# MLP down projection as seven half-size products per 1024 up columns (Strassen's scheme)

## The chip, the cores and the metric

The kernel runs on one core of one Trainium2 chip. The metric is the device time of one execution in microseconds (us). It is written in Bass, with every engine's instruction stream and every semaphore wait written out by hand. The engines are PE (TensorE, matmuls), PEld (its weight loads), DVE (VectorE), ACT (ScalarE), POOL (GpSimd) and SP (SyncE, which issues most DMAs).

## The reference

A decoder layer on 512 tokens of width 1024: three attention branches, a gated merge, cross-attention, and an MLP. The change touches the MLP alone. There `x` is (512, 1024), `mlp_w1` (1024, 4096) and `mlp_w2` (4096, 1024), all float32:

```python
h = rmsnorm(x, g[NORM_PRE_MLP])
x = x + rmsnorm(jnp.square(jax.nn.relu(h @ mlp_w1[l])) @ mlp_w2[l], g[NORM_POST_MLP])
```

## The kernel before, in words

Every dense product is done in three TensorE passes. Each float32 operand is split into a high part (rounded to the fp32r type) and a low part (the rest), and `blocks3` (L688 to L693) issues high times high, high times low and low times high for each 128-row chunk, all added up in PSUM. Each is a matmul of 128x128 stationary by 512 moving columns in most stages.

The weights come in slabs of 1 MB (128 partitions by 2048 columns). SP loads slab s into `raw[s % 2]` as soon as slab s-2 has been split (`load`, L640 to L643). ACT writes the high part (`high`, through the copy helper at L1333) into `wh[s % 2]` once TensorE is through with slab s-2, and VectorE subtracts it from the raw slab to give the low part (`low`, L1823 for slabs in halves or quarters, L1828 for whole ones) in `wl[s % 2]`. A "halved" slab is handed over in two halves, so that TensorE can begin on the first.

The MLP runs in two rounds (f = 0, 1) of 2048 up columns. A round has eight up slabs of 256 columns (48 matmuls each) and then eight down slabs (2 column halves of the output by 4 groups of 512 up columns, 48 matmuls each). For each up product ACT takes relu out of PSUM into `h1` (L1776), GpSimd squares it in place (L2463), ACT copies the high part to `h1H` (L1333, `up_high`), and VectorE writes the low part to `h1L` (L2355). ACT evicts the down products of round 0 to `yN`; VectorE adds those of round 1 (L2371). The row norm then follows for each 128-token tile: ACT squares and sums a half row (L1633), VectorE multiplies by the gain (L2374, L2390), adds the two sums (L2235), ACT takes the root (L1645), VectorE the reciprocal (L2377), and two fused multiply-adds (L2380, L2383) write the output rows that SP stores (L673).

Engines execute their streams strictly in the order written. So a wait in front of one instruction holds all that stand behind it on that engine. The order on VectorE in an up step is: low part of up slab n+2, then low part of up product n-1. ACT's is: relu of n, high part of slab n+2, high part of up product n-1.

Of the kernel before, what the change touches and what calls it, by code (L numbers as in the profile page):

```python
# [24 lines left out]
F32 = mybir.dt.float32  # L25
# [6 lines left out]
P = 128  # L32
# [49 lines left out]
def layer(nc, a, out):  # L82
# [11 lines left out]
    with ctx:  # L94
# [65 lines left out]
        gainPost = [at("gain_post0", [P, D], 172), at("gain_post1", [P, D], 180), at("gain_post2", [P, D], 176)]  # L160
        gainPre = [at("gain_pre0", [P, D], 176), at("gain_pre1", [P, D], 172)]
        squareJunk = at("square_junk", [P, D], 202)
        scaled = at("y_scaled", [P, NT, T], 160)
# [13 lines left out]
        h1H = at("up_high", [P, 16, T], 96, F32R)  # L177
        h1L = at("up_low", [P, 16, T], 128, F32R)
        h1 = at("up", [P, 2, 2, T], 160)
# [43 lines left out]
        CROSS = [S[0], PT, OT, S[1]]  # L223

# [105 lines left out]
        for f in range(2):  # L330
            for n in range(8):
                c = f * 2048 + n * SW
                slab(("up", f, n), square_slab(rows("mlp_w1"), c, c + SW))
            for n in range(2):
                for kk in range(4):
                    row_slab(("down", f, n, kk), rows("mlp_w2"), n, kk, f * 16)
# [3 lines left out]
        for s, pieces in enumerate(slabs):  # L340
            counts[s % 2] += 16 * len(pieces)
            landed.append(counts[s % 2])

# [5 lines left out]
                                              ("up", 0, 0), ("up", 0, 1))}  # L349
# [3 lines left out]
                                                        ("bp", 1, 3), ("nq", 0), ("kk", 0), ("vv", 0))})  # L353

# [123 lines left out]
        for f in range(2):  # L478
            for n in range(8):
                product(("up", f, n), "A", slab_at["up", f, n])  # L480
            for n in range(2):
                for kk in range(2):
                    part(slab_at["down", f, n, kk])
                if f == 0 or n == 0:
                    part(slab_at["down", f, n, 2])
                for t in range(NT):
                    if f == 1 and n == 1 and t == NT - 1:
                        part(slab_at["down", f, n, 2])
                    product(("down", f, n, t), "A" if f == 0 else "V", slab_at["down", f, n, 3])
# [14 lines left out]
        place_free[slab_at["up", 0, 1]] = used_at[slab_at["co", 1, 0]]  # L504
# [6 lines left out]
        def row_rank(name, n, t):  # L511

            return 4 * (t // 2) + 2 * n + t % 2 if name == ("co",) else NT * n + t
# [83 lines left out]
        gains2_loaded = sem("gain_rows_loaded_again")  # L597
        row_squared = [sem(f"row_squares{j}") for j in range(3)]
# [36 lines left out]
        def _(sp):  # L635
# [32 lines left out]
            for s in range(slab_at["cw", 0, 0], SLABS):  # L668
                load(s)
            for t in range(NT):  # L670
                for n in (1, 0):
                    sp.wait_ge(out_ready, 2 * t + 2 - n)
                    sp.dma_start(out_row(out)[:, t, n * T:(n + 1) * T], XN[:, t, n * T:(n + 1) * T]).then_inc(out_written, 16)  # L673
# [4 lines left out]
        def _(pe):  # L678
# [602 lines left out]
            def up_half(n, half, at_chunk=None):  # L1281

                c = slice(half * 2 * P, (half + 1) * 2 * P)
                act = (hTH[:, :, c], hTL[:, :, c])
                g = product_at["up", 0, n]
                dst = [G[g % 2][:, b, c] for b in range(2)]
                pe.wait_ge(taken["V"], taken_count[product_at["co", n, NT - 1]])
                return t_mode(slab_at["up", 0, n], dst, both, KD, act, at_chunk)
# [9 lines left out]
            up = (h1H, h1L)  # L1298
            for f in range(2):
                for n in range(0 if f else 2, 8):  # L1300
                    g = product_at["up", f, n]
                    if n < 2:
                        pe.wait_ge(taken["A"], taken_count[product_at["down", 0, 1, 2 * n + 1]])
                    else:
                        free(g)
                    t_mode(slab_at["up", f, n], two(g), both, KD, hT).then_inc(product_ready, 1)
                for n in range(2):
                    name = ("down", f)
                    together = f == 1 and n == 1
                    for kk in range(2 if together else 4):  # L1310
                        pe.wait_ge(up_ready, 8 * f + 2 * kk + 2)
                        for t in range(NT):
                            if kk == 0:
                                free_tile(name, n, t)
                            mm = rows_tile(slab_at["down", f, n, kk], name, n, t, up, 4 * kk, kk == 0, kk == 3)
                            if kk == 3 or t == NT - 1:
                                mm.then_inc(product_ready, 1)
                    if together:
                        for t, kk in ((0, 2), (1, 2), (0, 3), (1, 3), (2, 2), (2, 3), (3, 2), (3, 3)):
# [1164 lines left out]
```

## Time and profile before

| | us |
|---|---|
| median of 3 runs | 1449.33 |
| lowest and highest run | 1448.76, 1449.4 |
| span of the profiled execution, first to last instruction | 1447.3 |

The runs' time includes about 2.0 us around the span (1449.33 - 1447.3). The profile's page gives no other time for the profiled execution, so its own time is taken as its span and these 2.0 us.

| engine | busy us in the span | share |
|---|---|---|
| PE | 1435.3 | 99% |
| PEld | 1169.0 | 81% |
| DVE | 694.2 | 48% |
| ACT | 567.1 | 39% |
| POOL | 93.8 | 6% |

A matmul's listed duration reaches from its start until its result is out. Matmuls overlap, so what one of them costs in a full stream is the distance from one start to the next. The duration of a group on DVE or ACT is what an instruction takes, time in which it stands blocked after dispatch included.

### The profile page before, as it was taken

The numbers are of one execution on the slowest core, as the hardware profiler recorded it, in microseconds if no ns is written. First come the engines' busy times: TensorE is split into PE (matmuls) and PEld (weight loads), VectorE is DVE, ScalarE is ACT, GpSimd is POOL, SyncE is SP. The second block draws the span as 40 slices with busy tenths as digits, with TensorE's granted clock in tenths as the row PEclk, the third lists the DMA queues.
The fourth block names the chain that finished last, engine by engine and source line by source line (L and its number), as shares of the span: only waits on it lengthen the run. The fifth ranks groups of instructions, "written<-read, shape, count | busy, mean of one in ns | idle before, by whom it ended". The sixth has DMA issues, their size and how long they took to land.

```text
span 1447.3 us, 17264 instructions
## 1 busy us (share of the span) xinstructions
PE 1435.3 (99%) x7138; PEld 1169.0 (81%) x7138; DVE 694.2 (48%) x1194; ACT 567.1 (39%) x935; POOL 93.8 (6%) x70
## 2 busy tenths in 40 slices
PE   9999999999999999999999999999999999999998
PEld 7867778888888888877767888987789888888886
DVE  6477857854333454556155345563454232123234
ACT  4455541234334333355356234444434332233221
POOL 0000000023020000100000110000001110011100
PEclk9999999999999999999999999999999999999999
DMA  6211233223221245531100533452122322322321
GB/s 200 68 41 35 70 105 100 88 91 99 73 88 59 95 141 175 157 97 44 59 29 30 189 105 103 143 188 74 58 65 86 113 87 89 115 87 88 116 87 58
DMA packets 118144, 137.34 MB, mean 95 GB/s; under 512 B 7044, under 2 KB 98433, under 8 KB 118066
## 3 DMA queue, kind: packets, MB, share of 16 engines
q1 hardware_dynamic: 115216, 126.17, 27.2%
q0 software_dynamic: 2704, 10.00, 2.0%
q8 instruction: 57, 0.93, 0.3%
q14 instruction: 21, 0.17, 0.0%
q10 hardware_dynamic: 146, 0.07, 0.0%
HBM read 134.09 MB, written 2.14 MB: 94 GB/s over the span
## 4 chain that ended last, share of the span: by engine, by line
PE 98%; DVE 1%; ACT 0%; DMA 0%; issue 0%; DVEq 0%; ACTq 0%
PE dense L691 26%; PE dense L693 26%; PE dense L692 26%; PE score L837 4%; PE score L854 3%; PE turned L854 3%; PE turned L837 2%; PE turned L847 1%; PE score L847 1%; PE score L1008 1%; PE score L1009 1%; PE score L1231 0%; PE turned L1231 0%; PE score L1220 0%; PE turned L1220 0%; PE turned L819 0%
## 5 line engine op out<-in xcount | busy, mean ns | idle before, releaser
L1828 DVE TENSOR_TENSOR weight_low<-raw,weight_high 128x2048 fp32r<-128x2048 f32 (+2 forms) x96 | 200.2, 2092 | 356.1 <-ACT weight_high L1333 356.0
L691 PE MATMUL dense<-hidden_high,weight_high 128*128 128x512 f32 (+1 forms) x840 | 327.0, 389 | 0.0
L1333 ACT ACTIVATE weight_high<-raw 128x2048 fp32r<-128x2048 f32 (+5 forms) x172 | 222.2, 1323 | 259.9 <-PE dense L693 259.7
L693 PE MATMUL dense<-hidden_high,weight_low 128*128 128x512 f32 (+1 forms) x840 | 320.7, 382 | 0.0
L692 PE MATMUL dense<-hidden_low,weight_high 128*128 128x512 f32 (+1 forms) x840 | 320.3, 381 | 0.0
L693 PEld LDWEIGHTS dense<-hidden_high,weight_low 128*128 128x128 f32 x840 | 157.9, 188 | 30.9
L692 PEld LDWEIGHTS dense<-hidden_low,weight_high 128*128 128x128 f32 x840 | 158.2, 188 | 29.1 <-issue 0.5
L691 PEld LDWEIGHTS dense<-hidden_high,weight_high 128*128 128x128 f32 x840 | 158.1, 188 | 29.0 <-issue 0.5
L1823 DVE TENSOR_TENSOR weight_low<-raw,weight_high 128x1024 fp32r<-128x1024 f32 (+1 forms) x74 | 76.0, 1078 | 60.6 <-ACT weight_high L1333 60.6
L691 PE MATMUL dense<-weight_high,up_high 128*128 128x512 f32 x256 | 99.6, 389 | 0.0
L692 PE MATMUL dense<-weight_low,up_high 128*128 128x512 f32 x256 | 99.6, 389 | 0.0
L693 PE MATMUL dense<-weight_high,up_low 128*128 128x512 f32 x256 | 99.6, 389 | 0.0
L691 PE MATMUL dense<-weight_high,hidden_high 128*128 128x256 f32 (+1 forms) x288 | 82.0, 285 | 0.3 <-DVE hidden_low L1854 0.2
L693 PE MATMUL dense<-weight_high,hidden_low 128*128 128x256 f32 (+1 forms) x288 | 81.2, 282 | 0.0
L692 PE MATMUL dense<-weight_low,hidden_high 128*128 128x256 f32 (+1 forms) x288 | 81.2, 282 | 0.0
L691 PE MATMUL dense<-branch_out_high,weight_high 128*128 128x512 f32 x192 | 75.0, 391 | 0.0
L1446 ACT ACTIVATE probs<-probs,small 128x128 f32<-128x128 f32 (+3 forms) x128 | 70.2, 551 | 11.9 <-DVE small L1998 11.7
L693 PE MATMUL dense<-branch_out_high,weight_low 128*128 128x512 f32 x192 | 74.8, 389 | 0.0
L692 PE MATMUL dense<-branch_out_low,weight_high 128*128 128x512 f32 x192 | 74.7, 389 | 0.0
L1776 ACT ACTIVATE up<-dense 128x1024 f32<-128x1024 f32 x16 | 16.5, 1029 | 112.4 <-PE dense L693 112.4
L1333 ACT ACTIVATE probsT<-turned 128x512 f32<-128x512 f32 (+4 forms) x68 | 32.0, 471 | 71.5 <-PE turned L847 71.2
L837 PE MATMUL score<-kT,qT 128*128 128x128 f32 (+3 forms) x174 | 57.8, 440 | 0.7 <-ACT index_relu L1427 0.4
(341 smaller groups left out, 2288.9 us busy)
## 6 DMA issues: line engine op xcount, KB each, us to landing
raw<-in_w_in SPq DMA_DIRECT2D x33, 1024.0 KB, 5.2
raw<-in_mlp_w SPq DMA_DIRECT2D x32, 1024.0 KB, 5.1
raw<-in_w_branch SPq DMA_DIRECT2D x12, 1024.0 KB, 5.2
raw<-in_nsa_cmp_w SPq DMA_DIRECT2D x8, 1024.0 KB, 5.5
raw<-in_cross_wkv SPq DMA_DIRECT2D x8, 1024.0 KB, 5.4
raw<-in_w_in SPq DMA_DIRECT2D x11, 512.0 KB, 5.0
bias_strips<-bias_scratch POOLq DMA_DIRECT2D x8, 512.0 KB, 4.1
raw<-in_w_out SPq DMA_DIRECT2D x4, 1024.0 KB, 5.0
```

The source lines that it names most:

```text
L691: pe.matmul(out_ap, ah, bh, start=first, stop=False)
L692: pe.matmul(out_ap, ah, bl, start=False, stop=False)
L693: return pe.matmul(out_ap, al, bh, start=False, stop=last)
L837: mm = pe.matmul(SCORE[n % 3][:, 0:cols], q, k, start=j == 0, stop=j == len(terms) - 1)
L847: mm = pe.transpose(TURNED[m % 2][0:rows, (i - i0) * P:(i - i0 + 1) * P], probs_of(i), ident[:, :])
L854: mm = pe.matmul(ATT[att % 2][:, i0 * P:T], value, probsT[0:rows, m % 4, 0:T - i0 * P], start=first, stop=last)
L1008: pe.matmul(S[kv][:, 0:SW], flatS[kv][:, l:l + P], wh[s % 2][:, k, :], start=c + k == 0, stop=False)
L1333: return nc.scalar.activation(dst, src, ACT.Copy, scale=scale)
L1446: ins = nc.scalar.activation(t, t, ACT.Exp, bias=negmax[:, k:k + 1], scale=-1.0, accum_out=total[:, k:k + 1])
L1776: nc.scalar.activation(h1[:, n % 2, :, :], bank(("up", f, n))[:, :, :], ACT.Relu).then_inc(taken["A"], 1)
L1823: V.tensor_tensor(dst, src, hi.bitcast(F32), ALU.subtract).then_inc(low_ready, 1)
L1828: ins = V.tensor_tensor(dst, src, hi.bitcast(F32), ALU.subtract)
```

## The change

The down projection is cut into four segments of 1024 up columns. In a segment let A be the squared up activations (512 tokens by 1024) and B the weights (1024 by 1024), each cut into 2x2 quarters: A by token half and by the halves (b = 0, 1) of each up slab, B by interleaved row chunks and by output column half. Instead of eight products of quarters, seven are computed, of sums of quarters (Strassen's scheme in Winograd's form):

| form | activation | weight | added to the output quarter |
|---|---|---|---|
| 0 | a11 | b11 | (0,0), and `shared` |
| 1 | s1 = a21 + a22 | b12 - b11 | (0,1), (1,1) |
| 2 | s2 = s1 - a11 | b22 - (b12 - b11) | `shared` |
| 3 | a12 | b21 | (0,0) |
| 4 | s4 = a12 - s2 | b22 | (0,1) |
| 5 | s3 = a11 - a21 | b22 - b12 | (1,1), (1,0) |
| 6 | a22 | (b22 - b12 + b11) - b21 | subtracted from (1,0) |

`shared` is added to the quarters (0,1), (1,1) and (1,0) once, at the end of the last segment, by GpSimd.

What runs where:

- PE: per segment four up slabs as before, then seven forms by two token tiles by 4 chunks by 3 passes, 168 matmuls of 512 columns. The first two forms are run as chunks 0 to 2 of both forms and both tiles, and then chunk 3. The products go round four PSUM banks (`FORM`), and product n waits until product n-4 was taken.
- GpSimd, per segment: four squares as before and four weight sums of 128x2048, in this order: square 0, square 1, sum 0, square 2, sum 1, square 3, sum 2, sum 3. Sum 0 waits until VectorE has split up slab 4g+3 (whose raw place it writes to), sum 1 until it has split form 0's slab, sum 3 until it has split form 1's.
- VectorE, per up product: the low part of slab +2, four sums of 128x256 (`up_sums`), the low parts of three quarters and of four sums (`up_low`). Per form: one or two additions of 128x512 out of PSUM for each of its two tiles (`form_sums`), and the low part of slab +2, in halves (form 2 in quarters).
- ACT, per up product: relu, high part of slab +2, high parts of the three quarters (512 and 256 columns) and, after the sums, of the four sums (1024 columns).
- SP: the loads are written out by hand. The sums use three more raw places (`spareRaw`, at 176 KB and up), which lie over the residual rows; so these are written to HBM (2 MB) in the first segment and read back after the last up product. In the first segment the order is: up slab 0, up slab 1, up slab 2, write the rows and wait for it, quarters b11, b12, b22, then up slab 3.
- The row norm starts with output quarter (0,0) after form 3 and ends with quarter (1,0) after form 6.

The core of the diff:

```diff
+        formH = at("up_forms_high", [P, 7, 4, 2 * P], 96, F32R)
+        formL = at("up_forms_low", [P, 7, 4, 2 * P], 124, F32R)
+        h1 = at("up", [P, 2, 2, T], 152)
+        formS = at("up_sums", [P, 4, 2 * P], 160)
+        shared = at("down_shared", [P, 2, T], 164)
+        spareRaw = [at(f"down_raw{i}", [P, KD, SW], 176 + 8 * i) for i in range(3)]
...
+        halved |= {slab_at["form", g, i] for g in range(SEGMENTS) for i in range(FORMS)}
...
+        pieces_of.update({slab_at["form", g, 2]: 4 for g in range(SEGMENTS)})
...
@@ sync
+            for g in range(SEGMENTS):
+                if g:
+                    split_done(("form", g - 1, 3))
+                    sp.wait_ge(weights_summed, 4 * g)
+                else:
+                    sp.wait_ge(low_ready, split_at[FIRST_UP - 2])
+                load_up(4 * g)
...
+                load_up(4 * g + 1)
+                if not g:
+                    split_done(("up", 0))
+                    load_up(2)
+                    sp.wait_ge(hrow_ready[1], NT)
+                    sp.dma_start(kept, XN[:, :, :]).then_inc(spilled, 16)
+                    sp.wait_ge(spilled, 16)
+                    load_quarter(spareRaw[0], g, 0, 0, quarter_loaded[0])
+                load_quarter(spareRaw[1], g, 0, 1, quarter_loaded[1])
+                load_quarter(spareRaw[2], g, 1, 1, quarter_loaded[2])
+                if g:
+                    split_done(("up", 4 * g))
+                    load_up(4 * g + 2)
+                split_done(("up", 4 * g + 1))
+                load_up(4 * g + 3)
+                split_done(("up", 4 * g + 2))
+                load_quarter(upRaw[0], g, 1, 0, up_loaded[0])
+            sp.wait_ge(product_ready, ready_at["up", 15])
+            sp.dma_start(XA[:, :, :], kept).then_inc(x3_loaded, 16)
...
@@ tensor
+                for q in pairs:
+                    if q == 0 and n >= 4:
+                        pe.wait_ge(form_taken, n - 3)
+                    if t == 0 and q * pieces_of[s] % 4 == 0:
+                        slab_half(s, q * pieces_of[s] // 4)
+                    if t == 0 and i < 2:
+                        pe.wait_ge(up_ready, 2 * (4 * g + q) + i + 1)
+                    mm = blocks3(FORM[n % 4], (formH[:, FORM_ACT[i], q, c], formL[:, FORM_ACT[i], q, c]),
+                                 (high[:, q, :], low[:, q, :]), q == 0, q == 3)
...
@@ scalar
+            def up_split(u):
+                q = u % 4
+                act.wait_ge(up_squared, u + 1)
+                copy(formH[:, 0:2, q, :], h1[:, u % 2, :, 0:2 * P])
+                copy(formH[:, 2, q, :], h1[:, u % 2, 1, 2 * P:]).then_inc(up_high, 1)
+                act.wait_ge(up_summed, u + 1)
+                copy(formH[:, 3:7, q, :], formS[:, :, :]).then_inc(up_high, 1)
...
@@ vector
+            def up_sums(u):
+                dve.wait_ge(up_squared, u + 1)
...
+                V.tensor_tensor(formS[:, 0, :], a21, a22, ALU.add)
+                link(V.tensor_tensor(formS[:, 2, :], a11, a21, ALU.subtract))
+                link(V.tensor_tensor(formS[:, 1, :], formS[:, 0, :], a11, ALU.subtract))
+                V.tensor_tensor(formS[:, 3, :], a12, formS[:, 1, :], ALU.subtract).then_inc(up_summed, 1)
...
+            for g in range(SEGMENTS):
+                for u in range(4 * g, 4 * g + 4):
+                    low(slab_at["up", u] + 2)
+                    up_sums(u)
+                    up_low(u)
+                last = g == SEGMENTS - 1
+                form_sums(g, 0, 0)
+                low(slab_at["form", g, 0] + 2)
+                form_sums(g, 0, 1)
+                for i in range(1, FORMS):
+                    if last and i == 4:
+                        dve.wait_ge(gains3_loaded, 16)
+                        dve.wait_ge(x3_loaded, 16)
+                        for t in range(2):
+                            first_scale(0, t)
+                    for t in range(2):
+                        form_sums(g, i, t)
+                        if last and i == 4 and t == 0:
+                            finish_row(0)
...
+                    low(slab_at["form", g, i] + 2)
+                    if last and i == 4:
+                        finish_row(1)
...
@@ gpsimd
+                up_square(4 * g)
+                up_square(4 * g + 1)
+                for q in range(2):
+                    pool.wait_ge(quarter_loaded[q], 16 * (g + 1))
+                pool.wait_ge(low_ready, split_at[slab_at["up", 4 * g + 3]])
+                weight_sum(g, 0, other, b12, b11)
+                up_square(4 * g + 2)
+                pool.wait_ge(quarter_loaded[2], 16 * (g + 1))
+                pool.wait_ge(low_ready, split_at[slab_at["form", g, 0]])
+                weight_sum(g, 1, b11, b22, other)
+                up_square(4 * g + 3)
+                weight_sum(g, 2, b12, b22, b12)
+                pool.wait_ge(up_loaded[0], 16 * (3 * g + 3))
+                pool.wait_ge(low_ready, split_at[slab_at["form", g, 1]])
+                weight_sum(g, 3, other, b11, b21)
```

## Rows read from the trace of the kernel before

**Rows 1.** The page: busy time of each engine, and the chain that ended last.
```profile
PE 1435.3 (99%) x7138; PEld 1169.0 (81%) x7138; DVE 694.2 (48%) x1194; ACT 567.1 (39%) x935; POOL 93.8 (6%) x70
...
PE 98%; DVE 1%; ACT 0%; DMA 0%; issue 0%; DVEq 0%; ACTq 0%
```

**Rows 2.** Windows, MLP from up slab 2 on: length, busy us (instructions) of each engine.
```profile
1114.98:1440.94 325.96, 325.96 (x1439) 269.82 (x1438) 99.02 (x71) 94.69 (x86) 28.43 (x15) 1.00 0.29 96
```

**Rows 3.** Groups by form, 1100 to 1448 us: tiles, shape, count | busy, mean ns | idle before.
```profile
L691 PE MATMUL dense<-weight_high,up_high 128*128 128x512 f32 x256 | 99.6, 389 | 0.0
...
L2371 DVE TENSOR_TENSOR y_rows<-dense,y_rows 128x512 f32<-128x512 f32 x8 | 5.5, 690 | 11.3 <-PE dense L693 11.3
```

**Rows 4.** Groups by form, whole span: shapes that price the new pieces.
```profile
L1333 ACT ACTIVATE weight_high<-raw 128x1024 fp32r<-128x1024 f32 x49 | 49.3, 1049 | 22.1 <-PE dense L693 22.0
...
L1333 ACT ACTIVATE weight_high<-raw 128x512 fp32r<-128x512 f32 x32 | 17.6, 620 | 61.1 <-PE dense L693 61.1
...
L1998 DVE CUSTOM_DVE_ANT_0 probs<-score,bias_strips 128x256 f32<-128x256 f32 x12 | 5.1, 422 | 1.0 <-PE score L837 1.0
```

**Rows 5.** Timeline of one up step: start, us, engine, line, tiles.
```profile
1125.69 1.03 ACT L1776 ACTIVATE up<-dense 128x1024 f32<-128x1024 f32 x1 [7.13 <-PE dense L693]
1126.61 1.91 ACT L1333 ACTIVATE weight_high<-raw 128x2048 fp32r<-128x2048 f32 x1
...
1126.80 1.90 POOL L2463 TENSOR_TENSOR up<-up 128x1024 f32<-128x1024 f32 x1 [9.01 <-ACT up L1776]
...
1128.55 2.29 DVE L1828 TENSOR_TENSOR weight_low<-raw,weight_high 128x2048 fp32r<-128x2048 f32 x1 [7.48 <-ACT weight_high L1333]
```

**Rows 6.** Timeline at 486 us: a GpSimd sum and a VectorE subtraction.
```profile
485.86 2.39 POOL L2434 TENSOR_TENSOR merged<-merged,gated 128x1024 f32<-128x1024 f32 x1 [77.29 <-DVE gated L2083]
...
486.57 3.83 DVE L1828 TENSOR_TENSOR weight_low<-raw,weight_high 128x2048 fp32r<-128x2048 f32 x1 [0.78 <-ACT weight_high L1333]
```

**Rows 7.** Timeline at 534 us, and the same VectorE pair with GpSimd idle (1090 us).
```profile
534.26 4.55 DVE L1823 TENSOR_TENSOR weight_low<-raw,weight_high 128x1024 fp32r<-128x1024 f32 x2
...
534.43 3.30 POOL L2434 TENSOR_TENSOR merged<-merged,gated 128x1024 f32<-128x1024 f32 x1 [46.18 <-DVE gated L2083]
...
1090.11 2.35 DVE L1823 TENSOR_TENSOR weight_low<-raw,weight_high 128x1024 fp32r<-128x1024 f32 x2
```

**Rows 8.** Timeline at 299 us, and a GpSimd sum of the same size with VectorE idle.
```profile
299.09 2.43 DVE L1828 TENSOR_TENSOR weight_low<-raw,weight_high 128x2048 fp32r<-128x2048 f32 x1 [1.50 <-ACT weight_high L1333]
...
299.34 3.33 POOL L2423 TENSOR_TENSOR selection_strips<-bias_strips,selection_bias 128x512 f32<-128x512 f32 x1
...
304.28 1.27 POOL L2423 TENSOR_TENSOR selection_strips<-bias_strips,selection_bias 128x512 f32<-128x512 f32 x1
```

**Rows 9.** DMA issues: tiles, count, KB each, median us from issue to landing.
```profile
raw<-in_mlp_w SPq DMA_DIRECT2D x32, 1024.0 KB, 5.1
...
residual_rows<-in_x POOLq DMA_DIRECT2D x1, 2048.0 KB, 8.3
```

**Rows 10.** Windows 8 to 12 us: last column GB/s, before it the DMA share.
```profile
8.00:12.00 4.00, 3.71 (x25) 3.27 (x24) 3.70 (x5) 2.80 (x6) 0.00 (x0) 1.00 1.07 340
```

**Rows 11.** Timeline: last pre-MLP hidden rows, and ACT's relu of up product 1.
```profile
1097.90 1.29 DVE L2248 SCALAR_TENSOR_TENSOR y_rows<-residual_rows,small,gain_pre 128x1024 f32<-128x1024 f32 x1
...
1114.78 1.03 ACT L1776 ACTIVATE up<-dense 128x1024 f32<-128x1024 f32 x1 [2.93 <-PE dense L693]
```

**Rows 12.** Timeline of the end: last matmul, and VectorE's first and last step of the last row.
```profile
1440.78 0.39 PE L693 MATMUL dense<-weight_high,up_low 128*128 128x512 f32 x1
...
1441.21 0.69 DVE L2371 TENSOR_TENSOR y_rows<-dense,y_rows 128x512 f32<-128x512 f32 x1 [1.81 <-PE dense L693]
...
1444.08 0.75 DVE L2383 SCALAR_TENSOR_TENSOR residual_rows<-y_rows,small,residual_rows 128x512 f32<-128x512 f32 x1
```

**Rows 13.** Span and mean granted clock, and PE's longest wait.
```profile
core 0: 1447.3 us, clock 1.000
...
PE dense L744 <- DMA gain_row<-in_norm_gains: 2.8, 1, 2.8
```

More of the change, by code:

```diff
@@ L223, in layer @@
         CROSS = [S[0], PT, OT, S[1]]
+        FORM = [S[0], S[1], PT, OT]
         def flat(tile):
@@ L477, in layer @@
                         product(("co", n, t), "V", slab_at["co", n, 1])
[L478 to L489, printed above, removed]
+        for g in range(SEGMENTS):
+            for u in range(4 * g, 4 * g + 4):
+                product(("up", u), "A", slab_at["up", u])
+            for i in range(FORMS):
+                for t in range(2):
+                    part(slab_at["form", g, i] if t else None)
+                    ready_at["form", g, i, t] = events[0]
         held = {slab_at["co", 0, 0]: 0, slab_at["co", 1, 1]: 1}
@@ L511, in row_rank @@
         def row_rank(name, n, t):
+            if name == ("down",):
+                return 4 * (t // 2) + 2 * (n if t < 2 else 1 - n) + t % 2
             return 4 * (t // 2) + 2 * n + t % 2 if name == ("co",) else NT * n + t
@@ L1296, in _ @@
                 up_half(n, 1).then_inc(product_ready, 1)
[L1298 to L1319, printed above, removed]
-                            mm = rows_tile(slab_at["down", f, n, kk], name, n, t, up, 4 * kk, False, kk == 3)
-                            if kk == 3 or t == NT - 1:
-                                mm.then_inc(product_ready, 1)
@@ new lines, in _ @@
+            for g in range(SEGMENTS):
+                for u in range(4 * g if g else 2, 4 * g + 4):
+                    free(product_at["up", u])
+                    t_mode(slab_at["up", u], two(product_at["up", u]), both, KD, hT).then_inc(product_ready, 1)
+                for pairs in (range(3), range(3, 4)):
+                    for i in range(2):
+                        for t in range(2):
+                            form_pairs(g, i, t, pairs)
+                for i in range(2, FORMS):
+                    for t in range(2):
+                        form_pairs(g, i, t, range(4))
@@ new lines, in _ @@
+            for g in range(SEGMENTS):
+                for u in range(4 * g, 4 * g + 4):
+                    ready(("up", u))
+                    if u >= 2:
+                        act.wait_ge(up_ready, 2 * u - 2)
+                    nc.scalar.activation(h1[:, u % 2, :, :], bank(("up", u))[:, :, :], ACT.Relu).then_inc(taken["A"], 1)
+                    high(slab_at["up", u] + 2)
+                    up_split(u)
+                last = g == SEGMENTS - 1
+                if last:
+                    nc.scalar.activation(spare, eps, ACT.Sqrt)
+                for i in range(FORMS):
+                    if last and i == 4:
+                        for t in range(2):
+                            down_square(0, t)
+                    if last and i == 5:
+                        high(slab_at["form", g, 4] + 2)
+                        for t in range(2):
+                            down_square(1, t)
+                            row_root(2, t)
+                    if not (last and i == 4):
+                        high(slab_at["form", g, i] + 2)
@@ L1798, in _ @@
+            for t in range(2, NT):
+                down_square(1, t)
+            for t in range(2, NT):
+                down_square(0, t)
+                row_root(2, t)
         @block.vector
@@ L2231, in row_sum @@
             def row_sum(j, t):
-                dve.wait_ge(row_squared[j], row_rank((("wo",), ("co",), ("down", 1))[j], 1, t) + 1)
+                dve.wait_ge(row_squared[j], row_rank((("wo",), ("co",), ("down",))[j], 0 if j == 2 and t >= 2 else 1, t) + 1)
                 q = rowSquares[j]
```

258 lines of the change are left out of this document (162 added, 96 removed).

## The prediction

> **What bounds the kernel now.** I read the page first: PE is busy for 99% of the span and 98% of the chain that ended last is PE; VectorE has half its time free, ACT more, GpSimd nearly all [rows 1]. The window over the MLP from up slab 2 on holds 1439 matmuls in 325.96 us without a gap, so one costs 325.96 / 1439 = 0.2265 us of PE's time [rows 2]. The 389 ns that its group shows is the time until its result is out, and must not be used for the saving [rows 3]. So PE's own order is the bound; every matmul removed is worth 0.2265 us as long as nothing else makes PE wait. In 1447.3 us it has waited hardly at all, 2.8 us at most, at the start [rows 13]. The question is whether that stays so.
>
> **Matmuls removed.** The down projection had 16 slabs of 48 = 768 matmuls. Now there are 4 segments x 7 forms x 2 tiles x 4 chunks x 3 passes = 672. 96 x 0.2265 = **-21.7 us**. Nothing else leaves PE.
>
> **Work added, by totals.** Per segment PE has 4 x 48 x 0.2265 = 43.5 us of up and 168 x 0.2265 = 38.1 us of forms. VectorE has eleven slab splits at 2.29 (25.2) [rows 5], four times four sums of 256 columns at about 0.42 (6.7, from a two-operand operation of that size [rows 4]), four times the low parts of 1792 columns (about 2.3, so 9), and twenty 512-column additions out of PSUM at 0.69 (13.8) [rows 3]: 55 of 81.6 us. GpSimd has four squares at 1.90 [rows 5] and four sums of 2048 columns. Each engine alone has room. What decides is order, and one thing more.
>
> **GpSimd and VectorE shut each other out.** A 2048-column split takes 2.29 us; where GpSimd was inside a two-operand operation it took 3.83, and it ended 2.15 us after GpSimd's did (490.40 against 488.25), as if it had begun only then [rows 6]. Two half splits that take 2.35 us alone took 4.55, and GpSimd's 2.39 us operation took 3.30: GpSimd waited for the first half, ran, and the second half waited for it, though it stood right behind the first [rows 7]. At 299 us it went the other way round: VectorE's split ran, and GpSimd's 1.27 us operation took 3.33 [rows 8]. So for instructions with two SBUF operands they take turns, instruction by instruction, and whoever waits goes next. (VectorE's additions out of PSUM have one SBUF operand; I take them as free of it. No row shows them beside GpSimd.) Before, GpSimd did 1.90 us of squares per 10.9 us in a pause of VectorE [rows 5].
>
> **One segment in order.** Zero is the end of up product 4g+1. Products 4g+2 and 4g+3 take 10.9 us each, so the forms could begin at 21.6. Durations: relu 1.03, slab high part 1.91 (1.05 a half), slab split 2.29 (1.22 a half), square 1.90 [rows 4, 5]; 1024-column copies 1.05.
> - Slab 4g+3 is split at 5.2. VectorE starts its first 256-column sum, GpSimd weight sum 0 behind it: 5.45 to 10.05. VectorE's other three sums end at 11.25, ACT's copy of them at 12.35. ACT's relu of product 4g+2 stands behind that copy: to 13.3. Square to 15.4 (a low part goes first).
> - Form 0's split waits for the square: 15.3 to 17.65. Weight sum 1: 17.95 to 22.55. Three sums to 23.75, low parts of product 4g+2 to 24.8 and 26.1. ACT again comes late to relu 4g+3: to 25.8; its square to 27.95.
> - Form 1's first half is split at 29.05; weight sum 2 to 33.6; second half to 34.7; weight sum 3 from 35.0 to 39.6; three sums to 40.8; low parts of product 4g+3 to 41.8 (quarters) and 43.15 (sums).
> - PE: chunks 0 to 2 of the first four products wait for form 1's second half (34.7), and chunk 3 for 41.8. The four products end at 44.55. Without waits they end at 21.6 + 48 x 0.2265 = 32.45. So **+12.1 us**, four times: +48.4.
>
> The same chain with the weight sums out of the way gives low parts at 21.6 + 7.1 and 8.4, when chunk 3 is due at +8.15 and +9.5: no wait. So the sums' time is the cause, 4 x 4.6 = 18.4 us set in line.
>
> **Behind the four products.** They end 0.7 us apart and VectorE owes eight additions (5.3), form 2's split (2.4) and the first half of form 3's (1.2) before form 3 may start: 9.3 us after product 0, while PE has 7.4. **+2.0 us** per segment, +8. From form 3 on VectorE has 4.3 us of work per 5.4.
>
> **First segment.** Hidden rows are ready at 1099.2 [rows 11]; the 2 MB write, at the 8.3 us of a 2 MB read [rows 9], holds SP until 1107.6. Then three quarters and up slab 3 go into one queue: 4.2 MB, at 340 GB/s [rows 10] 12.3 us, so slab 3 lands at about 1121, at 5.1 us per MB [rows 9] at 1129. ACT would take it at 1115.7 [rows 11]. The whole chain above shifts by 5.4 us (2 to 13): **+5.4**.
>
> **Last segment and the end.** GpSimd's three additions of `shared` (2.39 each [rows 6]) alternate with the splits of forms 4 and 5: PE waits 0.3 and 1.5. Form 6's split stands behind `finish_row(0)`, which waits for ACT's square, which stands behind form 6's high part: PE waits 2.8. That is 4.6. Form 6's 24 matmuls (5.4 us) begin when the first half of its split is through, so 4.4 of them lie behind the split's end. From there VectorE has `finish_row(1)` 2.9, two double additions 2.6, form 6's first addition 0.65, two scalings 1.3, `finish_row(2)` 2.9, and an addition with `finish_row(3)` 3.6: 13.95, of which 13.95 - 4.4 = 9.6 come after the last matmul. Before, an addition and the same steps took 1441.21 to 1444.83, 3.6, ending 3.8 after PE's last slot (1440.78 + 0.23 = 1441.0) [rows 12]; 2.9 is 3.6 less the addition. **+4.6 + 5.8 = +10.4** (5 to 14).
>
> The read-back of the residual rows starts at the end of the last up product and has 25 us: nothing. If it were late, the end moves by that lateness.
>
> **Sum.** Span 1447.3 - 21.7 + 48.4 + 8 + 5.4 + 10.4 = 1497.8; with the 2.0 around it 1499.8, against the median of 1449.33. **1500 us, 3.5% slower.** Bounds: weight sum 3.8 us, -12.8, 4.8, +3; first segment -3.4, +7.6; end -5, +4; small gaps of the chain (0.1 at each of some twenty hand-overs per segment), +8.
>
> **Rivals.**
> 1. *No collision worth the name*: GpSimd's sums delay nobody. Then per segment 0.2 + 0.4 + 1.2 us of waits at forms 2 and 3 are left, 7.2 in all, 0.5 in the first and 7.5 in the last: 1449.3 - 21.7 + 15.2 = 1443. This is the faster side; it decides if a split beside a weight sum takes 2.3 us. Rows 6 to 8 speak against. Chance 0.07.
> 2. *VectorE goes first*: a queued VectorE instruction keeps GpSimd out until VectorE pauses. Then the sums slip into its waits for ACT; stalls of some 3.5 us per segment and 11 in first and last: 1449.3 - 21.7 + 14 + 11 = 1453. The second half in rows 7 speaks against. Chance 0.08, of which 0.03 within 0.2%.
> 3. *TensorE's clock falls in the waits.* The granted clock is 1.000, its 2.4 GHz level, throughout, but no wait there is over 2.8 us [rows 13]; here PE waits 4 us twice within 17. At the 1.2 GHz level a matmul costs 0.45; the 12 behind the second wait and form 2's 24 would cost 36 x 0.2265 = 8.2 more, of which the 2.0 above hides a part: +6 per segment, 1500 + 24 = 1524. The Trainium skill (TensorE: Matmul & The Clock Gate, Part 1) says that an idle engine falls back to that level; no row here shows it. Chance 0.13.
>
> **How the numbers follow.** Forecast 0.72, rivals 0.07, 0.08, 0.13. Range 1476 to 1526: the forecast's own bounds and rival 3 inside, rivals 1 and 2 left out. What a measurement of this kernel can tell from no change is about 0.2%. Faster by more: 0.07; within: 0.03; slower: 0.90.
>
> **What would show it.** PE should have the same 0.2265 us step, 96 fewer matmuls, and per segment two waits of about 4 us and several of 1 to 1.5 between the last up product and form 3; chunk 3 of the first products released by `up_low`. Half splits beside GpSimd should reach 3 to 6 us, 256-column sums one of 5, and the GpSimd sums 4.6. Wrong if the sums take well over 5 us (more loss), if VectorE's instructions keep their lengths (rival 1), or if up slab 3 is what PE waits for (first segment).

## The result, and the profile after

| | before | after |
|---|---|---|
| median (lowest to highest) | 1449.35 us (1448.76 to 1449.4) | 1498.6 us (1497.86 to 1498.94) |
| ratio, 95% interval | 1 | 1.034 (1.0326 to 1.0355) |
| span of the profiled execution | 1447.3 us | 1496.1 us |
| mean granted clock | 1.000 | 0.986 |

The change costs 49 us, 3.4%; the prediction said 1500. The page of the kernel after (busy us, share of the span, instructions; then the granted clock in 40 slices), against [rows 1]:

```profile
PE 1436.8 (96%) x7042; PEld 1159.7 (78%) x7042; DVE 889.5 (59%) x1413; ACT 604.1 (40%) x1010; POOL 182.5 (12%) x89
PEclk9999999999999999999999999999998999999999
```

The 96 matmuls are gone (7138 to 7042), yet PE is as busy as before: its busy time does not show the saving, because matmuls are listed longer where the clock had fallen, and the last one before each wait is listed with its full length. VectorE has gained 195 us of busy time. With the weight sums all but left out (the first experiment below) it gains 125 (818.9) for the same instructions of its own, so 71 us are time in which it stands still and is listed as busy. GpSimd has gained 89.

Where the time went, by PE's own order (start of the first matmul of a stage to that of the next). A form stage of 168 matmuls is worth 38.05 us by [rows 2].

| stage | us | over 38.05 |
|---|---|---|
| forms of segment 1 (1137.36 to 1193.62) | 56.26 | +18.2 |
| forms of segment 2 (1237.14 to 1289.40) | 52.26 | +14.2 |
| forms of segment 3 (1332.92 to 1385.37) | 52.45 | +14.4 |
| forms of segment 4 (1428.89 to 1485.15) | 56.26 | +18.2 |

Up stage 2 takes 43.52, as its 192 matmuls want; up stage 1 is 0.7 late; and from PE's last slot to VectorE's end are 8.4 instead of 3.8, +4.6. The sum: -21.7 + 0.7 + 18.2 + 14.2 + 14.4 + 18.2 + 4.6 = 48.6, and the spans differ by 48.8. So nearly all of it lies in the form stages and at the end.

What PE waits for there, in the view of waits of the kernel after from 1080 us on (line waited for: us in total, times, longest):

```profile
PE score L772 <- DVE up_forms_low L2466: 11.5, 4, 6.4
PE score L772 <- DVE weight_low L1919: 10.1, 6, 3.8
PE turned L772 <- DVE weight_low L1919: 9.8, 5, 3.8
PE turned L772 <- DVE up_forms_low L2466: 7.7, 4, 2.5
```

39 us, all of it for VectorE (3.6 more are listed as issue), where the kernel before had nothing to wait for. Why VectorE is late stands in the timeline of segment 2 of the kernel after (start us, us, engine, line, tiles, in brackets the idle time before and its releaser), from two stretches:

```profile
1218.44 2.29 DVE L1924 TENSOR_TENSOR weight_low<-raw,weight_high 128x2048 fp32r<-128x2048 f32 x1 [4.65 <-ACT weight_high L1420]
1220.65 0.41 DVE L2456 TENSOR_TENSOR up_sums<-up 128x256 f32<-128x256 f32 x1
1220.90 4.63 POOL L2632 TENSOR_TENSOR raw<-down_raw,down_raw 128x2048 f32<-128x2048 f32 x1 [2.32 <-DVE weight_low L1924]
1220.98 4.82 DVE L2457 TENSOR_TENSOR up_sums<-up 128x256 f32<-128x256 f32 x1
...
1242.03 7.67 DVE L1919 TENSOR_TENSOR weight_low<-raw,weight_high 128x1024 fp32r<-128x1024 f32 x2 [0.64 <-ACT weight_high L1420]
1243.11 5.51 POOL L2632 TENSOR_TENSOR down_raw<-down_raw,down_raw 128x2048 f32<-128x2048 f32 x1
...
1249.75 0.61 PE L772 MATMUL score<-weight_high,up_forms_high 128*128 128x512 f32 x1 [3.79 <-DVE weight_low L1919]
1249.83 4.61 POOL L2632 TENSOR_TENSOR raw<-down_raw,raw 128x2048 f32<-128x2048 f32 x1 [1.21 <-DVE weight_low L1919]
1249.95 4.77 DVE L2457 TENSOR_TENSOR up_sums<-up 128x256 f32<-128x256 f32 x1
...
1256.64 0.66 PE L772 MATMUL turned<-weight_high,up_forms_high 128*128 128x512 f32 x1 [2.28 <-DVE up_forms_low L2466]
```

Two equal 256-column sums stand one behind the other on VectorE: the first takes 0.41 us, the second 4.82. GpSimd's weight sum starts at 1220.90, beside the first. The second sum is then listed from 1220.98 to 1225.80, 0.27 after the end of GpSimd's 4.63 us. It is no slower an instruction; it stands still. The two half splits of form 1 (2.35 alone [rows 7]) take 7.67, with GpSimd's 5.51 in their middle, of which 0.9 is GpSimd's own wait for the first half. PE's matmul at 1249.75 has waited 3.79 us for that pair, and the one at 1256.64 another 2.28 for the low parts behind the last sum.

### The profile page after: what moved, and what is told of

Its sections match the earlier page's. It is cut to its first block and busy times, and to the rows that moved or that the text cites. A ratio compares the mean times of both kernels' runs of the same rounds, so it can differ in the third digit from the quotient of the medians.

```text
span 1496.1 us, 17514 instructions
## 1 busy us (share of the span) xinstructions
PE 1436.8 (96%) x7042; PEld 1159.7 (78%) x7042; DVE 889.5 (59%) x1413; ACT 604.1 (40%) x1010; POOL 182.5 (12%) x89
## 5 line engine op out<-in xcount | busy, mean ns | idle before, releaser
L1420 ACT ACTIVATE weight_high<-raw 128x1024 fp32r<-128x1024 f32 (+5 forms) x183 | 215.9, 1217 | 205.9 <-PE dense L774 168.3
L1924 DVE TENSOR_TENSOR weight_low<-raw,weight_high 128x2048 fp32r<-128x2048 f32 (+2 forms) x77 | 156.6, 2042 | 192.9 <-ACT weight_high L1420 192.9
L1919 DVE TENSOR_TENSOR weight_low<-raw,weight_high 128x1024 fp32r<-128x1024 f32 (+1 forms) x104 | 132.6, 1322 | 64.5 <-ACT weight_high L1420 64.5
L772 PE MATMUL score<-weight_high,up_forms_high 128*128 128x512 f32 x112 | 48.4, 432 | 24.1 <-DVE up_forms_low L2466 11.5
L772 PE MATMUL turned<-weight_high,up_forms_high 128*128 128x512 f32 x112 | 48.0, 429 | 18.8 <-DVE weight_low L1919 9.8
L1420 ACT ACTIVATE up_forms_high<-up_sums 128x1024 fp32r<-128x1024 f32 x16 | 16.9, 1059 | 115.7 <-DVE up_sums L2459 115.7
L2457 DVE TENSOR_TENSOR up_sums<-up 128x256 f32<-128x256 f32 x16 | 59.3, 3703 | 0.0
```

The source lines that it names most:

```text
L772: pe.matmul(out_ap, ah, bh, start=first, stop=False)
L1420: return nc.scalar.activation(dst, src, ACT.Copy, scale=scale)
L1919: V.tensor_tensor(dst, src, hi.bitcast(F32), ALU.subtract).then_inc(low_ready, 1)
L1924: ins = V.tensor_tensor(dst, src, hi.bitcast(F32), ALU.subtract)
L2457: link(V.tensor_tensor(formS[:, 2, :], a11, a21, ALU.subtract))
```

## The experiments

Times are medians, ratios are to the kernel before on the same chip (its medians there: 1449.2 to 1449.3 us).

**Is it the weight sums, and is it their length?** The same program with each weight sum cut to 8 of its 2048 columns, and then to half (here and below the signal at the end of each line is not shown):

```
-  Q.tensor_tensor(dst[:, :, :],   a[:, :, :],   b[:, :, :],   ALU.subtract)
+  Q.tensor_tensor(dst[:, 0, 0:8], a[:, 0, 0:8], b[:, 0, 0:8], ALU.subtract)   # e1_tiny_sums
+  Q.tensor_tensor(dst[:, 0:4, :], a[:, 0:4, :], b[:, 0:4, :], ALU.subtract)   # e2_half_sums
```

> GpSimd's sixteen weight sums are cut to 8 of 2048 columns; every wait and signal stays. Left out: most of the weight sums, so forms 1, 2, 5 and 6 multiply raw or stale slabs. Collision (GpSimd's sums and VectorE's two-operand instructions shut each other out): the form stages lose only 0.2 + 0.4 + 1.2 us each instead of the 18.2, 14.2, 14.4 and 18.2 of the changed kernel, so about 1498.6 - 54 = 1444 us (1441 to 1448); VectorE's second 256-column sum of each up product takes 0.42 us instead of 4.8; the granted clock is 1.000. Rival, late loads or ACT's order set the waits: over 1480.

> The weight sums are cut to 1024 of 2048 columns, all waits kept. Left out: half of each weight sum. A GpSimd sum then takes 2.4 us instead of 4.6. Collision, with the four sums of a segment in one line with VectorE's work: 16 x 2.2 = 35 us less and some of the slow clock gone, 1458 to 1465. Rival, only one or two of the four sums matter (the others lie beside work that waits for something else): 1475 to 1485.

Measured: e1 1445.5 us, 0.9974 (0.9964 to 0.9984); e2 1465.39, 1.0111 (1.0095 to 1.0126), 0.4 above its range. The form stages take 40.07, 40.07, 40.08 and 43.9 in e1, 47.7, 44.05, 44.08 and 49.5 in e2. The second 256-column sum, as a group (count | busy, mean ns | idle before), in the kernel after:

```profile
L2457 DVE TENSOR_TENSOR up_sums<-up 128x256 f32<-128x256 f32 x16 | 59.3, 3703 | 0.0
L2459 DVE TENSOR_TENSOR up_sums<-up,up_sums 128x256 f32<-128x256 f32 x16 | 6.8, 425 | 0.6
```

in e1:

```profile
L2457 DVE TENSOR_TENSOR up_sums<-up 128x256 f32<-128x256 f32 x16 | 6.7, 419 | 0.0
```

and in e2:

```profile
L2457 DVE TENSOR_TENSOR up_sums<-up 128x256 f32<-128x256 f32 x16 | 33.1, 2067 | 0.0
```

Twelve of the sixteen executions of that line stand beside a weight sum (the first product of a segment has none), and its mean follows the sum's length: 0.42, 2.07, 3.70 us for sums of 0, 2.4 and 4.6. So the weight sums cost 1498.6 - 1445.5 = 53 us; all the rest of the change together is worth -4. The loss is not quite proportional: the first 2.4 us of a sum cost 20 us in all, the next 2.2 cost 33, which is near the full 16 x 2.2 = 35. What slack VectorE has may cover some of the first part (not tested by itself), and the fall of the clock told of below belongs to the second: in e2 the mean clock is 0.997, in the kernel after 0.986. That e1 still has 2.0 us too much per form stage is the term "behind the four products", seen by itself.

**GpSimd busy, or GpSimd reading?** Two fills in place of the sum, which keep GpSimd busy and write the same tensor but read nothing from SBUF; and a copy, which reads one tensor instead of two:

```
-  Q.tensor_tensor(dst[:, :, :], a[:, :, :], b[:, :, :], ALU.subtract)
+  Q.memset(dst[:, :, :], 0.0)                                # e3_memset, twice in a row
+  Q.tensor_copy(dst[:, :, :], (a if dst is not a else b)[:, :, :])    # e8_copy_sums
```

> Each weight sum is replaced by two fills of the same 2048 columns, one after the other, about 4.2 us of GpSimd (from 0.53 us for 512 columns), which read nothing. Left out: the weight sums. If what hurts is that GpSimd's operation reads SBUF while VectorE reads two operands: VectorE's instructions keep their lengths, 1444 to 1450. If any GpSimd access shuts VectorE out, or if GpSimd's occupied time itself delays the squares behind it: 16 x 0.4 = 6 us less than the changed kernel, about 1492.

> Each weight sum is replaced by a copy of one of its operands (2048 columns), all waits kept. Left out: the other operand of each weight sum. Separates reading at all from reading two operands. If any GpSimd instruction that reads SBUF keeps VectorE's two-operand instructions out for its length L, the time lies between the runs with fills (1445.6) and whole sums (1498.6) by 16 L: with L near 2.4 as in the run with half sums, about 1465. If only two operands on both sides collide: 1445.5 whatever L is.

Measured: e3 1445.58 us, 0.9975 (0.9965 to 0.9985), the time of e1; e8 1459.78, 1.0073 (1.0059 to 1.0087). In e3 a fill takes 1.81 us, the two 3.6, less than the 4.2 expected, but still long against a 0.42 us sum. Its timeline, with the same second 256-column sum (L2457 above is L2458 in this file):

```profile
1216.70 1.81 POOL L2633 MEMSET down_raw<- 128x2048 f32 x1 [2.33 <-issue]
...
1216.85 0.41 DVE L2458 TENSOR_TENSOR up_sums<-up 128x256 f32<-128x256 f32 x1
```

The instruction that stood still for 4.82 us runs through in 0.41 beside a GpSimd instruction that only writes. In e8 the copy takes 1.93 us, and the sum beside it 2.12:

```profile
1210.61 1.93 POOL L2632 COPY raw<-down_raw 128x2048 f32<-128x2048 f32 x1 [2.31 <-DVE weight_low L1924]
1210.70 2.12 DVE L2457 TENSOR_TENSOR up_sums<-up 128x256 f32<-128x256 f32 x1
```

One tensor read is enough to keep VectorE out for the whole instruction. The time follows the duration: 1445.5 at none, 1459.8 at 1.93, 1465.4 at 2.4, 1498.6 at 4.6. (The 1465 expected of e8 was for a copy of 2.4 us.) So neither GpSimd's lateness is the cause (in e3 it is occupied for 3.6 us each time and costs nothing against e1) nor its writing.

**The first segment.** Up slab 3 in the queue ahead of the residual rows' write and the quarters:

```
   # SyncE, first segment, right after load_up(2)
+  split_done(("up", 1)); load_up(3)      # and not at its later place
```

> In the first segment SP loads up slab 3 ahead of the write of the residual rows and the three quarters. Term of the sum 'first segment': in the changed kernel slab 3 lands at 1121.9, the up stage ends 0.7 us late and the first form stage is 4 us longer than the second (18.2 against 14.2 over 38.05). With the early load: 1498.6 - 4.7 = 1494 (1493 to 1495), first form stage 52.3 us. Rival, the first stage is longer for another reason (its copies, the DMA traffic): 1497.5 to 1498.6.

Measured: 1494.1 us, 1.0308 (1.0294 to 1.0323): the time that was expected, though not all from the place expected. In the kernel after ACT had to wait for that slab:

```profile
1121.89 1.92 ACT L1420 ACTIVATE weight_high<-raw 128x2048 fp32r<-128x2048 f32 x1 [4.19 <-DMA raw<-in_mlp_w]
```

With the edit that wait is gone (the slab's high part starts at 1117.86), the up stage has its usual length, and the form stage takes 54.35 instead of 56.26. I had expected it to come down to the 52.3 of the middle ones. The 2.1 left have another cause by the order of ACT's work, which the prediction had missed and no run takes away by itself: the first two up products of the first segment end only 5.8 us apart (ACT's relus at 1109.0 and 1114.8 in the kernel before; 10.9 apart elsewhere), so ACT still owes the copy of product 0's sums when product 1 is ready, its relu starts at 1116.95, and the whole chain begins that 2.1 later. Of the 3.8 us by which the profiled execution is shorter, 2.7 lie in the first segment, where 4.7 were expected, and 1.2 in the last form stage and the end together. These 1.2 are no gain of the edit: in the last segment the matmuls behind the wait for form 0's last low parts happened to run at the full clock (at 1.2 GHz in the kernel after), and everything behind them is that much earlier. VectorE is through 6.9 us after PE's last slot instead of 8.4 only because PE's form 6 ran slowly there (next section); from form 6's split to VectorE's end it is 15.4 us in both.

**Does the clock take a part?** Behind the two long waits the clock was down. Windows of the kernel after (length; busy us and instructions of PE, PEld, DVE, ACT, POOL; granted clock; DMA share; GB/s), in the long wait, behind it, and behind the second one:

```profile
1245.80:1249.60 3.80, 0.16 (x1) 0.00 (x0) 3.80 (x1) 0.00 (x0) 2.81 (x1) 1.00 0.00 0
1249.70:1253.20 3.50, 3.45 (x9) 2.66 (x10) 3.50 (x2) 0.00 (x0) 3.37 (x1) 0.54 0.00 0
1256.60:1260.00 3.40, 3.36 (x8) 2.69 (x9) 2.51 (x3) 0.61 (x2) 0.00 (x0) 0.53 0.00 0
```

After PE stood still for 3.8 us it was granted 0.54 of full speed, its 1.2 GHz level for all but the edges of the window, and a matmul costs 0.43 us there instead of 0.2265. Counted from start to start, 61 matmuls of the four form stages are that slow, 22, 16, 12 and 11 by stage: 12 us more than at full speed. PE's busy time is 20 us larger (1436.8 us, where a version without long waits, the last one below, has 1416.6 for the same 7042 matmuls); it also counts the 0.16 us by which a matmul's listed time exceeds its slot, once at each of 22 waits. With the 39 us of waits for VectorE and 3.6 listed as issue these 20 make 63 of the 65 us by which the four form stages are too long. To see what that is worth, PE was given idle work to do while it waits: transposes of the identity matrix into a free bank, which nobody reads.

```
   # TensorE, before form 1's third chunk, form 0's fourth (and form 0's third in segment 1)
+  for _ in range({(1, 2): 30, (0, 3): 18, (0, 2): 50}[i, q]):
+      pe.transpose(G[k % 2][:, 0, 0:P], ident[:, :], ident[:, :])
```

> TensorE runs idle 128x128 transposes (18 to 50 of them) while it waits for form 1's second half and for up_low of the last product, so that it is never idle for 4 us. The granted clock should stay 1.000 there. Theory, the slow stretches lie mostly beside waits for VectorE: only the 12 matmuls behind the last wait hand over their products earlier, 0.7 us per segment, 1495 to 1497. Rival, every slow matmul costs its extra 0.2 us (some 22 per segment): 1498.6 - 18 = 1481.

Measured: 1497.07 us, 1.0332 (1.0318 to 1.0346). The same two stretches in that kernel:

```profile
1249.70:1254.00 4.30, 3.73 (x21) 2.94 (x20) 4.30 (x3) 0.00 (x0) 3.08 (x2) 1.00 0.01 4
1256.60:1261.00 4.40, 3.07 (x12) 2.10 (x12) 4.21 (x8) 2.43 (x4) 0.00 (x0) 1.00 0.00 0
```

The clock is 1.00 in both, and the median is 1.5 us lower, which is hardly more than the spread of the runs (1496.31 to 1498.94 against 1497.86 to 1498.94; the two intervals overlap). The stages say more. The two middle ones, where no matmul is slow any more, are 1.0 and 1.2 us shorter. In the first, 7 matmuls stay slow and it is 0.2 longer; in the last, 15 stay slow and it is 1.4 longer. So the edit holds the clock in two stages of four. From its 1.0 and 1.2 I estimate 4 to 5 us for the clock in all four, of the 49. The clock falls, as rival 3 said, but costs little: behind the first fall PE waits for VectorE anyway, and a slow matmul only eats a part of the next wait.

The last stage is longer because form 6 starts at 0.43 us a matmul there. No idle work had been put before it, and the wait is the same as in the kernel after, where the clock stays up. The same happens in e4. Form 6's first matmul in the kernel after, and in e4:

```profile
1479.59 0.47 PE L772 MATMUL turned<-weight_high,up_forms_high 128*128 128x512 f32 x1 [2.14 <-DVE weight_low L1919]
1475.86 0.76 PE L775 MATMUL turned<-weight_high,up_forms_high 128*128 128x512 f32 x1 [2.14 <-DVE weight_low L1922]
```

This costs the kernel nothing: PE's last slot comes 1.5 us later, VectorE's end does not (it lies 6.8 us behind that slot in e7, 8.4 in the kernel after).

**The weight sums on VectorE.** They are worth 16 x 2.29 = 36.6 us there, and VectorE is free for more than that. Placed in its pauses (two behind the low parts of product 4g+1, one behind those of 4g+2, one with form 2), with GpSimd left to do squares and the additions of `shared`:

```
   # VectorE, after up_low(u)
+  if u % 4 == 1: weight_sum(g, 0, upRaw[1], spareRaw[1], spareRaw[0])
+                 weight_sum(g, 1, spareRaw[1], spareRaw[2], spareRaw[1])
+  if u % 4 == 2: weight_sum(g, 2, spareRaw[0], spareRaw[2], upRaw[1])
   # and with form 2
+                 weight_sum(g, 3, upRaw[1], spareRaw[0], upRaw[0])
```

> All work kept: the four weight sums of a segment go to VectorE (2.29 us each), two behind up product 4g+1, one behind 4g+2, one behind form 4's split; GpSimd keeps the squares and the additions of shared. Collision: VectorE works 9.2 us more per segment, yet PE waits less: 1449.4 - 21.7 + 0.7 + 4.4 (first segment, late up slab 3) + 3 x 1.8 + 3.5 (last) + 4.6 (end) + 1 = 1447 (1444 to 1452). Rival, VectorE's total work in these segments is what PE waits for: at or over 1498.6.

Measured: 1457.59 us, 1.006 (1.0043 to 1.0077). 41 us better than the change, and 10 worse than I expected. The first and the last form stage have most of that: they are 9.1 and 11.4 us over 38.05 (4.4 and 3.5 expected), the middle ones 2.8 each (1.8 expected). I had moved the sums and looked only at them. Their new neighbours are GpSimd's other instructions:

```profile
1219.65 3.38 POOL L2645 TENSOR_TENSOR up<-up 128x1024 f32<-128x1024 f32 x1 [8.99 <-ACT up L1870]
...
1221.20 4.05 DVE L1919 TENSOR_TENSOR weight_low<-down_raw,weight_high 128x1024 fp32r<-128x1024 f32 x2
...
1419.15 13.35 POOL L2652 TENSOR_TENSOR y_rows<-y_rows,down_shared 128x1024 f32<-128x1024 f32 x3 [17.30 <-DVE down_shared L2503]
...
1424.66 5.59 DVE L1919 TENSOR_TENSOR weight_low<-down_raw,weight_high 128x1024 fp32r<-128x1024 f32 x2
```

A square that takes 1.90 alone [rows 5] takes 3.38, since it waits for VectorE's 2.29 us sum, and then holds up form 0's split (4.05 for 2.35). At the end three additions of `shared` take 13.35 for 7.2 and stretch form 5's split to 5.59, on which PE waits 0.9 us, and the two scalings behind it to 3.48 for 1.28; form 6's split stands behind these and the rows' finish, and PE waits 4.4 us for it. What the first stage owes to the late slab 3 and what to its neighbours was not taken apart.

**No GpSimd beside VectorE at all.** First without the squares: ACT squares in place (1.05 us each), up slab 3 is loaded first, form 3's split stands ahead of the last addition of form 1, and `finish_row(0)` and `finish_row(1)` stand behind form 6's split. Then, on top, the additions of `shared` on VectorE as well:

```
   # ScalarE, after the high part that follows the relu                 (e6, e9)
+  nc.scalar.activation(h1[:, u % 2, :, :], h1[:, u % 2, :, :], ACT.Square)
   # VectorE                                                            (e6, e9)
+  if i == 1 and t: low(slab_at["form", g, i] + 2)
-  if last and i == 4 and t == 0: finish_row(0)
   low(slab_at["form", g, i] + 2)
+  finish_row(0)
   finish_row(1)
   # VectorE: add_shared(0, 1) early, these two behind form 6's split   (e9)
+  add_shared(1, 1); add_shared(1, 0)
   # GpSimd
-  up_square(u), weight_sum(...)      (e6, e9)       - the additions of shared (e9)
```

> All work kept. The weight sums on VectorE as in the run before, and beside it: the squares on ACT (GpSimd keeps only the three additions of shared), up slab 3 loaded first, form 3's split ahead of the last addition of form 1, both rows' finish behind form 6's split. With GpSimd out of the way up to the last forms, stages 1 to 3 should take 38.5 to 39.5 us of an ideal 38.05, the last 44 to 46, the end 8.4 us after the last matmul as in the changed kernel: 1449.4 - 21.7 + 3 x 0.8 + 7 + 4.6 = 1442 (1438 to 1446), below the kernel before. Rival, the collision was not what kept the run before at 1457.6: no better than 1452.

> All work kept. As e6_reordered, but VectorE also adds shared (three times 128x1024, 1.2 us each) and GpSimd does nothing in the MLP. In e6_reordered GpSimd's three additions lengthened form 5's split from 2.35 to 5.58 us and a scaling from 1.28 to 3.47, and PE waited 1.8 and 1.6 us for it. Without them the last form stage should take 39.5 us instead of 42.6, and the end grows, since VectorE is never free from form 0 on: 1442.1 - 1 = 1441 (1440 to 1442). Rival, VectorE's 3.7 us more come out whole at the end: 1442.5 to 1443.

Measured: e6 1442.1 us (1442.01 to 1442.36), 0.9951 (0.9938 to 0.9965), as expected (its edits went in together, and their shares were not measured apart); e9 1439.57 (1439.47 to 1440.13), 0.9933 (0.992 to 0.9947), 0.4 below the range expected (the last form stage took 38.8, not 39.5) and the fastest of all, 9.6 us ahead of the kernel before and 59 ahead of the change. Its page:

```profile
PE 1416.6 (99%) x7042; PEld 1152.3 (80%) x7042; DVE 845.2 (59%) x1432; ACT 620.4 (43%) x1026; POOL 63.4 (4%) x54
```

And a window of its second segment, most of it the form stage (columns as above):

```profile
1216.00:1259.61 43.61, 43.37 (x191) 35.37 (x190) 37.98 (x47) 19.57 (x23) 0.00 (x0) 1.00 0.32 110
```

VectorE is busy for 38.0 of 43.6 us, GpSimd for none, and PE has no gap worth the name. VectorE did more work than in the kernel after (sixteen sums and three additions more) with 44 us less busy time (845.2 for 889.5): what is missing is time in which it stood still. Form stages: 38.81 three times and 38.8 in the last, +0.76 each over the ideal. From form 6's last matmul to the end it is 12.8 us, where the kernel before has 3.8. -21.7 + 4 x 0.76 + 9.0 = -9.7, and -9.6 was measured.

## Why the prediction was right, step by step

1. **-21.7 for 96 matmuls.** Confirmed by bookkeeping that closes within 0.2 us, in the change (48.6 against 48.8) and in e9 (-9.7 against -9.6).
2. **GpSimd and VectorE take turns, instruction by instruction.** Right in mechanism and in its pieces: weight sums 4.56 to 4.67 (forecast 4.6), third one 5.5 (it waits for the first half), the second 256-column sum 4.8 ("one of 5"), the pair of form 1 7.67 (forecast 27.85 to 34.7, 6.9). e1, e2, e3 and e8 show the cause by taking it away and by halving it. Rivals 1 and 2 are out: without the collision the kernel takes 1445.5 (e1; rival 1 said 1443), and VectorE's queued instruction does not keep GpSimd out.
3. **+12.1 up to the end of the four products.** Segment 2: the last up product ends at 1237.15, the four products at 1261.07, 23.9 later, and 48 x 0.2265 = 10.9 was due: +13.05. The order is as worked out, chunk 3 released by `up_low` included. About 1.1 of it is the slow clock, which the term left out: in e7, with the clock held, the four products take 22.9.
4. **+2.0 behind them** was +1.05, as PE, a little later than forecast, had less to wait for. The two together are 14.1, by an error of +1 and one of -1.
5. **First segment +5.4.** Its excess over a middle one is 0.7 + 18.2 - 14.2 = 4.7. The late slab has 2.6 of it (0.7 in the up stage and 56.26 - 54.35 by e4), the close ends of the first two up products 2.1, of which I knew nothing: ACT was ready for slab 3 at 1117.7 (forecast 1115.7) and got it at 1121.9 (forecast 1121). So 4.7 against 5.4 is partly luck: one cause was smaller than forecast, the other stood in no term.
6. **Last segment and end, +4.6 and +5.8.** The stage measured 18.2 - 14.2 = 4.0 over a middle one, of which PE's waits at forms 5 and 6 are 1.08 and 2.14 (forecast 1.5 and 2.8, and 0.3 at form 4), and the end measured 4.6. The additions of `shared` do alternate with the splits. Timeline of the kernel after, GpSimd's three and VectorE beside them:

```profile
1461.58 2.35 DVE L1919 TENSOR_TENSOR weight_low<-down_raw,weight_high 128x1024 fp32r<-128x1024 f32 x2
1461.73 10.16 POOL L2655 TENSOR_TENSOR y_rows<-y_rows,down_shared 128x1024 f32<-128x1024 f32 x3 [15.51 <-DVE down_shared L2497]
1463.84 0.68 DVE L2497 TENSOR_TENSOR y_rows<-score,y_rows 128x512 f32<-128x512 f32 x1
1465.20 0.69 DVE L2497 TENSOR_TENSOR y_rows<-score,y_rows 128x512 f32<-128x512 f32 x1 [0.67 <-PE score L774]
1466.35 6.63 DVE L1919 TENSOR_TENSOR weight_low<-down_raw,weight_high 128x1024 fp32r<-128x1024 f32 x2 [0.46 <-ACT weight_high L1420]
```

7. **VectorE's additions out of PSUM are free of it.** Assumed without a row; the fence above has it. GpSimd's first addition is let in when the split ends, at about 1463.9, and with its 2.39 us [rows 6] runs to about 1466.3 (the single times are not listed; the three take 10.16, 7.2 of work and the first's 2.2 of waiting among it). The two additions out of PSUM at 1463.84 and 1465.20 lie in that stretch and take 0.68 and 0.69 us, as ever [rows 3].
8. **Rival 3, the clock.** Its condition came true, but it counted more slow matmuls than there are (36 per segment, 144; measured 61), and above all had the wrong price for them: +6 per segment, where e7 gives 1.0 and 1.2 back. The step that failed was to add them to a chain that is set by VectorE. Where PE has to wait for somebody again, slow matmuls are paid from the wait.

My own miss behind the prediction, e5, is the same mistake in the other direction: I priced an instruction by where it had been, not by what it would stand beside.

## What to carry to other kernels

GpSimd is no spare engine beside a VectorE on whose results the critical engine waits: here each GpSimd instruction that read SBUF cost VectorE its whole length when VectorE had work with two SBUF operands queued, however short that was, so a 4.6 us sum that VectorE does in 2.29 is dearer on GpSimd than on VectorE. Before moving elementwise work, list for each side what it will stand beside, and look for an instruction of fixed shape whose duration varies: the excess is the neighbour's length. An edit that removes matmuls is worth their slots only if every producer keeps its distance, and that is found by writing out one segment in order, not from busy shares: VectorE was 59% busy in the worst and in the best version.

## What the runs showed of the hardware

- GpSimd's **reading** of SBUF is what excludes VectorE's instructions with two SBUF operands. A copy of 2048 columns (1.93 us) holds a 0.42 us sum for 2.12; two fills of the same tensor (1.81 each) hold nothing, 0.41. This I had not known from the rows of the kernel before, where every GpSimd instruction that met one of VectorE's read something. The Trainium skill (SBUF — State Buffer, section "SBUF: two separate sides") says so: VectorE's operation with two SBUF inputs and a GpSimd operation that reads SBUF hold a shared port pair exclusively, for the whole instruction. These runs agree, the copy and the fills as much as the free additions with one PSUM operand.
- Who waits goes next: of two VectorE instructions queued back to back, the first is let through and GpSimd goes in between (7.67 us for a pair of 2.35).
- Durations on fp32 in SBUF, 128 partitions. GpSimd: sum of two tensors of 2048 columns 4.6 us, copy 1.93, fill 1.81, square of 1024 in place 1.90; VectorE's sum of 2048 2.29, ACT's square of 1024 1.05.
- After a wait of 3.8 us PE was granted its 1.2 GHz level (0.54 over a window that includes its edges; 0.43 us a matmul instead of 0.2265); in the kernel before, with waits of 2.8 at most, the mean clock was 1.000. The length of the wait alone does not decide: before form 6 of the last segment PE stands still for 2.14 to 2.18 us in the kernel after, e1, e2, e3, e4, e7 and e8, and matmuls behind that run at 0.43 us in e2, e4, e7 and e8 only. In the two form stages where it was held up by idle work this gave 1.0 and 1.2 us back.
